# Delta preparation: the weight tile's load of each SyncE round put ahead of the heads' transfers

## What is computed

```python
gcum = jnp.cumsum(gc, axis=-1)
decay = jnp.exp(jnp.where(tri, gcum[..., :, None] - gcum[..., None, :], -jnp.inf))
kb = kc * bc[..., None]
m = jnp.where(strict, jnp.einsum('nbhik,nbhjk->nbhij', kb, kc) * decay, 0.0)
t_inv = lax.linalg.triangular_solve(m + eye, ...)          # unit lower triangular
attn = jnp.einsum('nbhik,nbhjk->nbhij', qc, kc) * decay
# and q_i * jnp.exp(g_i), used by the scan over the chunks
```

## Time and profile before

| | |
|---|---|
| median of 3 runs | 4231.96 us (4227.57 to 4232.15) |
| profiled execution | 4233.49 us |
| its span, first to last instruction | 4231.6 us |
| TensorE busy | 4114.4 us, 97% of the span |
| mean granted TensorE clock | 0.986 |
| `delta_prepare`, first `high` to the last low matmul | 936.9 to 1260 us |

### The profile page before, as it was taken

One profiled execution on the slowest core, in us unless ns is written; L12 is line 12 of the kernel. 1 busy time (PEld: TensorE's weight loads), 2 busy tenths in 40 slices (PEclk: granted clock), 3 DMA queues, 4 the chain that ended last, 5 costly groups with the idle time before them and its releaser, 6 DMA issues. The chain is left out here.

```text
span 4231.6 us, 66226 instructions
## 1 busy us (share of the span) xinstructions
PE 4114.4 (97%) x24351; PEld 3594.3 (85%) x24351; DVE 2981.2 (70%) x5007; ACT 1980.1 (47%) x2942; POOL 319.5 (8%) x654
## 2 busy tenths in 40 slices
PE   8999999999988999999999999999999999999999
PEld 1888888779988999888888888888888888888899
DVE  5778885966866677578876665666666568876746
ACT  1542223537653344444455554444444465454644
POOL 0000000000566600000000000000000100300000
PEclk9999999999999999999999999999999899999999
DMA  9673433468864357556765566777777455454564
GB/s 380 232 273 130 155 138 126 151 220 292 271 215 132 103 206 269 188 184 211 211 195 182 180 183 204 243 242 241 240 242 243 158 178 173 155 166 156 176 195 159
DMA packets 271301, 846.31 MB, mean 200 GB/s; under 512 B 74192, under 2 KB 112352, under 8 KB 234736
## 3 DMA queue, kind: packets, MB, share of 16 engines
q1 hardware_dynamic: 271088, 843.40, 60.6%
HBM read 792.85 MB, written 50.45 MB: 199 GB/s over the span
## 5 line engine op out<-in xcount | busy, mean ns | idle before, releaser
L231 DVE TENSOR_TENSOR rounded<-arena,rounded 128x1024 fp32r<-128x1024 f32 x792 | 976.9, 1234 | 495.6 <-ACT rounded L225 493.7
L225 ACT ACTIVATE rounded<-arena 128x1024 fp32r<-128x1024 f32 x792 | 840.0, 1061 | 770.1 <-DMA arena<-in_peer_v 355.4
L2500 PE MATMUL bank<-rounded,rounded 128*128 128x512 f32 x2048 | 524.5, 398 | 0.0
L3352 PE MATMUL bank<-rounded,rounded 128*128 128x512 f32 x1856 | 473.7, 397 | 4.4 <-DVE rounded L3797 2.9
L2500 PEld LDWEIGHTS bank<-rounded,rounded 128*128 128x128 f32 x2048 | 367.1, 189 | 65.9
L2891 PE MATMUL bank<-rounded,rounded 128*128 128x512 f32 x1024 | 399.7, 390 | 4.0 <-PEq L151 4.0
L2892 PE MATMUL bank<-rounded,rounded 128*128 128x512 f32 x1024 | 399.4, 390 | 0.0
L3352 PEld LDWEIGHTS bank<-rounded,rounded 128*128 128x128 f32 x1856 | 335.0, 190 | 66.1 <-issue 4.5
L2505 PEld LDWEIGHTS bank<-rounded,rounded 128*128 128x128 f32 x2048 | 279.0, 189 | 21.5 <-DVE rounded L231 0.3
L2505 PE MATMUL bank<-rounded,rounded 128*128 128x256 f32 x2048 | 285.2, 282 | 0.0
L2895 PE MATMUL bank<-rounded,rounded 128*128 128x512 f32 x1024 | 274.5, 390 | 0.0
(11 more groups left out here) (507 smaller groups left out, 7807.2 us busy)
## 6 DMA issues: line engine op xcount, KB each, us to landing
arena<-in_w_in SPq DMA_DIRECT2D x128, 1024.0 KB, 5.0
arena<-in_peer_u SPq DMA_DIRECT2D x256, 512.0 KB, 3.9
arena<-in_peer_v SPq DMA_DIRECT2D x256, 512.0 KB, 4.4
arena<-in_w_in SPq DMA_DIRECT2D x232, 512.0 KB, 3.6
arena<-in_w_mod SPq DMA_DIRECT2D x80, 1024.0 KB, 7.6
arena<-in_w_out SPq DMA_DIRECT2D x48, 512.0 KB, 3.6
arena<-in_w_conv_out SPq DMA_DIRECT2D x16, 1024.0 KB, 4.9
arena<-in_w_dn_out SPq DMA_DIRECT2D x16, 1024.0 KB, 5.1
```

The lines of the kernel that those rows point to most:

```text
L225: act.activation(k.half(0, r, q), k.raw_half(r, q), ACT.Copy).then_inc(k.hi_done, 1)
L231: dve.tensor_tensor(k.half(1, r, q), k.raw_half(r, q), k.half(0, r, q), ALU.subtract).then_inc(k.lo_done, 1)
L2500: pe.matmul(k.ps[r][:], part(0, m), flat(k.r(pair_slot + 2 * kt, 2)), start=(kt == 0), stop=False, skip_group_check=True)
L3352: pe.matmul(both, part(0, m), hi_lo(kt), start=(kt == 0), stop=False, skip_group_check=True)
```

## The change

In each round the load of tile j, with its wait, is moved from behind the heads' transfers to ahead of them. Nothing is added or taken away, and no other engine's code is touched. In the changed file the load is line 1350, the matrix store 1357, the store of `aq` 1362.

```diff
             for j in range(tiles):
+                if j >= 2:
+                    sp.wait_ge(k.lo_done, 2 * (s + j - 2) + 2)
+                    sp.dma_start(k.raw(j % 2), w[j]).then_inc(k.raw_loaded[j % 2], 16)
                 for i in (2 * j - 5, 2 * j - 4):
                     for h in at_half(i, 2):
                         if h + 2 < HEADS:
@@
                         sp.wait_ge(masked, h + 1)
                         sp.wait_ge(qg_done, h + 1)
                         sp.dma_start(scratch["aq"][h], aq[h % 2]).then_inc(aq_out[h % 2], 16)
-                if j >= 2:
-                    sp.wait_ge(k.lo_done, 2 * (s + j - 2) + 2)
-                    sp.dma_start(k.raw(j % 2), w[j]).then_inc(k.raw_loaded[j % 2], 16)
                 if 17 <= j < 21:
                     blocks_in(1, [j - 17])
                     blocks_in(0, [j - 17])
```

## The result

| | before | changed |
|---|---|---|
| median | 4232.06 us (4227.57 to 4233.65, 4 runs) | 4270.25 us (4267.18 to 4270.82, 4 runs) |
| ratio | | 1.009 [1.0078, 1.0102] |
| span of the profiled execution | 4231.6 us | 4268.8 us |
| mean granted clock | 0.986 | 0.983 |

The changed kernel is slower by 38.2 us. The forecast was 4260 us in a range of 4244 to 4275: the direction and the place were right, the loss was taken 10 us too small.

A forecast was written before the change was run, and what follows sets the result against it. TensorE, busy 97% of the span, was taken as the bound, so only its idle time matters. Stalls of 27.6 us plus 4.2 for the clock minus 4.0 won gave +27.8 us, 4260 us, range 4244 to 4275.

The forecast's parts named there:

- The bound and the sign: TensorE 97% busy, little to win; 41 of 46 loads issued at their buffer's release, so load first makes the kernel slower.
- The `aq` store as the urgent one: Heads 0 to 5: `row_exp(h+2)` needs it two halves later; rows needed after two or three halves, matrix store six.
- The pitch: Head to head, heads 0 to 5: 15.0 or 15.1 us instead of 9.97, five steps losing about 5.05 us each.
- The even heads' landing: Heads 0, 2, 4: `aq`, second behind the weight load after a row load, lands 9.3 us after the load's issue.
- The way from an even head's `row_exp` to the next load: From an even head's landing through `high`, TensorE's half, `high` and `low` to the next load's release: 7.0 us.
- The gaps' sizes: TensorE gaps ahead of halves 11, 14, 17, 20, 23, 26: about 2.4 us, then 4 to 5 us.
- The clock: Gaps of 5 us lower it; counts behind heads 2, 4 and the last stall: 3 x 1.4 = 4.2 us.
- Rounds 19 and 21: Late loads of tiles 19 and 21 come earlier with the 1 MB behind them: 4.0 us won, bounds 0 and 4.2.
- From head 6 on nothing: From head 6, `row_exp(h+2)` comes three halves or more after the low part the load awaits: loss taken as 0.
- The not-slower mechanism: Rival: `aq` lands in time, within 2.8 us of the load's issue at head 1; 4228 us; chance 0.12.
- The short queue: Rival: emptier queue in stalled rounds, landings at the low pair (6.2 and 7.6 us); 13 to 17 us, 4247; chance 0.14.
- The long stall: Rival: landings of 9.0 and 10.4 us, long low clock, nothing won; 42 us, 4274; chance 0.06 together with late heads.

The follow-up runs named there:

- e1: Changed kernel, but the `aq` store put back ahead of the load; rows and matrix store stay behind it: 4239.04 us, ratio 1.0017.
- e10: Changed kernel, but ScalarE issues the `aq` stores of heads 0 to 5 on its own queue at half base+7: 4234.32 us, ratio 1.0007.
- e4: Kernel before, with the load first only in rounds 8, 11 and 14 (`aq` stores of heads 1, 3, 5): 4252.74 us, ratio 1.0045.
- e9: Changed kernel, with `row_exp` of heads 0 to 7 called one half later on ScalarE: 4243.89 us, ratio 1.003.
- e6: Kernel before, with the load first in rounds 19 and 21 alone: 4229.83 us, ratio 0.9999.
- e3: Kernel before, with the load first only from round 17 on: 4229.31 us, ratio 0.999.

## Why the prediction was right, and where it was off

- **The bound and the sign: right.** 41 loads went out at their release, so going first could not speed them, and it did not (53.3 us of waits for tiles, 41.8 before). The pool the change could win from was as small as read from the earlier trace rows.
- **The `aq` store as the urgent one: right, shown by e1 and e10.** In e10 only the place and the queue of its issue changed, and the loss fell from 38.2 us to 1.9 by the medians and 3 by the ratio, which is not clear of none. Of the rows and matrices I had said that they are needed later; that is true but not free: e1 lost 7 us with them behind the load. The forecast had no term for this. In the changed kernel it is not a term on top (39.0 against 37.5) but acts through the landing times below.
- **The pitch: the failed step.** I had 15.0 us from an even head to an odd one and 15.1 back. Measured are 18.5, 18.4 and 17.8, and 14.2 twice. The three steps from an even head to an odd one are 9.7 us longer than forecast. The term most mis-sized is "the first store is there after 0.4 + 7.6 = 8.0 us", with 5.8 of them; the other 3.8 are the way from `row_exp` to the next load, below. These are the changed kernel's issues of SyncE in rounds 7 and 8, and the time to landing of the load and the `aq` store of round 8 (KB, us):

```profile
982.63 0.33 SPq L1350 DMA_DIRECT2D arena<-in_w_in  x1
983.01 0.42 SPq L1357 DMA_DIRECT2D delta_m<-arena  x1
983.53 0.38 SPq L1326 DMA_DIRECT2D arena<-delta_g  x1
987.83 0.33 SPq L1350 DMA_DIRECT2D arena<-in_w_in  x1
988.26 0.38 SPq L1362 DMA_DIRECT2D delta_aq<-arena  x1
```

```profile
arena<-in_w_in SPq DMA_DIRECT2D x1, 1024.0 KB, 9.1
```

```profile
delta_aq<-arena SPq DMA_DIRECT2D x1, 512.0 KB, 10.0
```

  From the load's issue that is 0.4 + 10.0 = 10.4 us, and 9.6 and 9.7 in rounds 11 and 14. After head 0's stall ScalarE and VectorE catch up, low parts follow each other closely, and rounds 7 and 8 are issued 5.2 us apart: 2 MB were issued in the 5.2 us ahead of the load of round 8, and the load among them landed 0.7 us after it had gone out. The pattern that I took the 8.0 from had a load 5.8 us and 0.5 MB 2.2 us ahead of it, and e4 shows that 8.0 and the gap of 5.2 are right for an odd stall that stands alone. e9, with these rounds 7.4 to 9.7 us apart, has it near 8 again. I had changed the pitch of the chain without asking what the new pitch does to the queue.
- **The even heads' landing: too long.** Head 0's landed after 9.2 us, as forecast (9.3). But behind an odd stall of 11 us the queue is nearly empty (DMA share 0.29 in the stretch from 994.0), and `aq` is there 8.3 us after the load's issue at 1004.11 and at 1036.71, not 9.3. From the landing to that issue it took 5.8 us, exactly as worked out. The two steps from an odd head to an even one so came out 0.9 us shorter each.
- **The way from an even head's `row_exp` to the next load: too short.** It took 8.06, 8.63 and 8.06 us instead of 7.0. The sum led over TensorE's half; behind a stall it is ScalarE and VectorE that work without a break, on the heads as well. VectorE in the changed kernel, the low parts of halves 12 and 13 and between them the matrix of head 2, which the sum did not have:

```profile
984.32 1.22 DVE L1564 TENSOR_TENSOR rounded<-arena,rounded 128x1024 fp32r<-128x1024 f32 x1
985.46 1.22 DVE L1582 SCALAR_TENSOR_TENSOR arena<-bank,arena 128x1024 f32<-128x1024 f32 x1
986.59 1.21 DVE L1564 TENSOR_TENSOR rounded<-arena,rounded 128x1024 fp32r<-128x1024 f32 x1
```

- **The account of the steps.** Head 0: 2.1 (forecast 2.4). Five steps: 83.12 - 5 x 9.97 = 33.3 (forecast 25.2). Clock behind the last stall: 1.9. Together 37.3, against a slip of 37.5.
- **The gaps' sizes.** I had said 2.4 and then 4 to 5 us; they alternate between some 8 and some 2. An even step loses 14.2 - 9.97 = 4.2 us, but only 2.06 show as a gap at half 17. The rest is TensorE at 0.50 after the gap of 8.40 at half 14, which brings it to half 17 late. So the slow clock behind an odd stall is free only as long as the chain is longer, as forecast, and it hides idle time that would be there without it.
- **The clock: nearly right.** Forecast 4.2 on the chain. From the rows: 21 matmuls in 4.49 us at 1064.6, where at full clock 28 take 3.4 and 21 would take 2.55, so 1.9 us; at half 17, 19 matmuls in 3.40 instead of 2.3, so 1.1. That is 3.0; by the low clock it fell behind only one even stall of the two.
- **Rounds 19 and 21: 2.7 us, not 4.0.** The bound "SyncE remains held up behind the blocks of the round before" was the truth. The hold-up had been on the rows and on the matrix store. Before, in rounds 19 and 20:

```profile
1055.42 2.99 SPq L1326 DMA_DIRECT2D arena<-delta_g  x1
...
1062.21 5.35 SPq L1354 DMA_DIRECT2D delta_m<-arena  x1
```

  and in the changed kernel it is on the loads:

```profile
1093.72 3.73 SPq L1350 DMA_DIRECT2D arena<-in_w_in  x1
...
1100.93 4.63 SPq L1350 DMA_DIRECT2D arena<-in_w_in  x1
```

  Hence the new gap at half 40.
- **From head 6 on nothing: right.** From half 26 to 37 the slip stands at 37.8. The five further waits of L1456 are 4.3 us together and make no gap.
- **The rest of the 10 us.** On the spans, +37.2: 27.8 forecast, 5.5 more in heads 0 to 5 with their clock (37.3 for 31.8), 1.3 less won, 2.2 between half 44 and the end of the stage; what is left is 0.4. The 2.2 I did not trace: in e6, which differs from before in two rounds only, the same stretch came out 4.4 us longer and the time did not change.
- **The rivals.** The not-slower mechanism fell at head 1, whose `aq` landed 10.4 us after the load's issue and not within 2.8. The short queue holds for no odd head, and the even ones lie between its 7.6 and my 9.3. The long stall's landing of 9.0 us was exceeded by the odd heads, but its sum of 42 was not reached, since the even heads stayed below its 10.4. That 9.0 was never read from a row: the first store behind the load at 1243.30 took 7.6 us, 8.0 from the load. So the upper bound of the range had a term that its own pattern does not show, and that the time fell within owes something to terms off in both directions. The Trainium skill's rule for a transfer, "DMA: Bandwidth & Descriptors", section on fixed and variable cost, gives about 4.4 us for 1 MB; it is fitted there to transfers that go through GpSimd's path, while these are SyncE's. Here a load took 5.9 at 982.63 and 9.1 at 987.83, so it holds for neither.

## What to carry to other kernels

A transfer that already goes out the moment its buffer is free is not sped up by going first in an in-order queue. Such an order puts the others behind its wait as well as its bytes, so look for the one among them with the tightest reader; it goes ahead of the wait or on another engine's queue. When a stall is to be priced, take the landing time at the spacing that the stall makes, not at today's: engines that catch up bunch the transfers behind it.

## What the hardware showed that I had not expected

- The same load of 1 MB on the same queue took 5.9 us from issue to landing with little ahead of it and 9.1 with 2 MB issued in the 5.2 us before it.
- Issuing a transfer right behind the 32x32x32 block fetches held SyncE for 2.2 to 5.4 us in the kernel before, the changed one and e3, where an issue takes 0.3 to 0.4; the hold-up stays where the blocks are and hits whatever is next. In e6 the load of tile 19 escaped it, at 0.35 us, and the rows behind it took 1.36.
- With gaps of 4.8 to 8.4 us in these kernels the granted clock went to 0.50, already within the gap, and stayed there for 3.4 to 10.2 us. A gap of 1.31 us (half 23) had none behind it, and one of 2.06 (half 17), itself behind such a stretch, was followed by 3.4 us of it.
